# Mixture-of-experts weights: sixteen neighbouring rows of the gate and up matrices to a partition, in one 32 KB run

## What is computed

```
xn2 = rms_norm(x) * g_ffn
group  = argmax(softmax(xn2 @ w_router_group + b))            # 1 of 4 groups
e1, e2 = top2(softmax(xn2 @ w_router_expert + b) in group)    # 2 of its 8 experts
for each expert e, its tokens xb:                             # 32 experts
    hdn = silu(xb @ w_gate[e]) * (xb @ w_up[e])               # [2048 x 512] each, 4 MB each
    y   = hdn @ w_down[e]                                     # [512 x 2048], 4 MB
x += weighted sum of each token's two expert rows
```

## Time and profile before

| | us |
|---|---|
| median of 3 runs | 3235.22 |
| lowest, highest | 3231.18, 3235.81 |
| span of the profiled execution | 3231.3 |
| busy in the span: TensorE / VectorE / ScalarE | 2907.9 / 585.5 / 345.4 |

### The profile page before, as it was taken

How to read it: one execution, slowest core, us unless ns; L and a number is a source line. 1 busy time by engine, 2 the same in 40 slices (tenths; PEclk the granted TensorE clock), 3 DMA queues, 4 the chain that set the end, 5 groups by cost and what they waited for, 6 DMA issues and landing times.

```text
span 3231.3 us, 34069 instructions
## 1 busy us (share of the span) xinstructions
PE 2907.9 (90%) x14086; PEld 1892.7 (59%) x14086; DVE 585.5 (18%) x1118; ACT 345.4 (11%) x573; POOL 51.0 (2%) x76
## 2 busy tenths in 40 slices
PE   3989899999999999999999968888888888887697
PEld 2556565555555555555558865555545554554586
DVE  3243424224433000000000030000000000010311
ACT  2121121212222000000000010000000000000101
POOL 1000000000000000000000000000000000000000
PEclk8999999999999999999999969999999999999799
DMA  6252443322323333333333249999999999998422
GB/s 140 84 163 70 144 133 107 114 91 84 110 84 104 104 104 100 96 95 98 103 131 119 69 153 391 401 392 399 400 399 400 397 397 398 402 397 311 149 78 91
DMA packets 359592, 646.61 MB, mean 200 GB/s; under 512 B 7789, under 2 KB 196709, under 8 KB 340261
## 3 DMA queue, kind: packets, MB, share of 16 engines
q1 hardware_dynamic: 340944, 600.06, 52.0%
q0 software_dynamic: 6528, 27.54, 3.1%
q10 hardware_dynamic: 12090, 18.62, 1.6%
HBM read 616.16 MB, written 30.04 MB: 200 GB/s over the span
## 4 chain that ended last, share of the span: by engine, by line
PE 79%; DMA 14%; DVE 4%; issue 1%; ACT 1%; ACTq 0%; DVEq 0%; POOL 0%; POOLq 0%; SPq 0%
PE bank L1236 20%; PE bank L1135 13%; DMA arena<-in_w_exp_up_dram 12%; PE bank L1314 11%; PE bank L1206 8%; PE bank L1298 6%; PE bank L1348 5%; PE bank L1259 5%; PE bank L1332 4%; PE bank L1100 1%; DVE arena L886 1%; PE bank L1190 1%; DMA arena<-in_conv_r_w_dram 1%; PE bank L1350 1%; DMA arena<-in_state_ssm_dram 1%
## 5 line engine op out<-in xcount | busy, mean ns | idle before, releaser
L1236 PE MATMUL bank<-arena 128*128 128x384 f32 x2048 | 660.6, 486 | 0.0
L1314 PE MATMUL bank<-arena 128*64 128x256 f32 x4096 | 489.8, 402 | 109.6 <-DMA arena<-in_w_exp_up_dram 67.5
L1236 PEld LDWEIGHTS bank<-arena 128*128 128x128 f32 x2048 | 389.1, 190 | 271.4
L1314 PEld LDWEIGHTS bank<-arena 128*64 128x64 f32 x4096 | 313.2, 145 | 296.3 <-DMA arena<-in_w_exp_up_dram 74.7
L1135 PE MATMUL bank<-arena 128*128 128x384 f32 x1280 | 416.3, 488 | 0.0
L1135 PEld LDWEIGHTS bank<-arena 128*128 128x128 f32 x1280 | 243.9, 191 | 170.0 <-issue 3.3
L1206 PE MATMUL bank<-arena 128*128 128x384 f32 x1024 | 331.7, 486 | 3.0 <-ACT arena L570 3.0
L1206 PEld LDWEIGHTS bank<-arena 128*128 128x128 f32 x1024 | 194.3, 190 | 140.0 <-ACT arena L570 4.9
L1332 PE MATMUL bank<-arena 128*64 128x512 f32 x1024 | 230.1, 602 | 28.7 <-DVE arena L1046 25.1
L1298 PE MATMUL bank<-arena 128*128 128x128 f32 x1632 | 189.2, 278 | 9.2 <-DVE arena L1020 9.2
L1298 PEld LDWEIGHTS bank<-arena 128*128 128x128 f32 x1632 | 186.0, 194 | 15.5 <-issue 15.5
(11 more groups left out here) (287 smaller groups left out, 1350.5 us busy)
## 6 DMA issues: line engine op xcount, KB each, us to landing
arena<-in_w_exp_gate_dram SPq DMA_DIRECT2D x32, 4096.0 KB, 20.1
arena<-in_w_exp_up_dram SPq DMA_DIRECT2D x32, 4096.0 KB, 23.3
arena<-in_w_exp_down_dram SPq DMA_DIRECT2D x32, 4096.0 KB, 22.8
arena<-in_w_in_dram SPq DMA_DIRECT2D x48, 2048.0 KB, 8.3
arena<-in_w_out_m_dram SPq DMA_DIRECT2D x8, 2048.0 KB, 8.1
arena<-in_w_out_r_dram SPq DMA_DIRECT2D x8, 2048.0 KB, 8.1
arena<-in_w_o_dram SPq DMA_DIRECT2D x8, 2048.0 KB, 8.2
expert_rows<-arena ACTq DMA_DIRECT2D x64, 256.0 KB, 6.9
```

The lines of the kernel that those rows point to most:

```text
L1236: last = mm(banks[2 * s + cc][:, 0:T], slab[s % 2][:, k, cc * 128:(cc + 1) * 128], rhs[:, k, :], start=(k == 0), stop=(k == KC - 1))
L1314: last = mm(banks[2 * x + i][h * SLOTS:(h + 1) * SLOTS, 0:FF // 2], xe[:, k, x * SLOTS:(x + 1) * SLOTS], w[:, k, h * (FF // 2):(h + 1) * ( ...
```

## The change

Partition p now takes rows 16p to 16p+15 of the gate and up matrices, which lie next to each other in HBM: one run of 32 KB instead of 16 runs of 2 KB. The down matrix is loaded as before. Block k of the contraction then holds channels k, 16+k, 32+k and so on, so the tokens' channels must be permuted to match: the scaling of the three tiles of the second norm reads its source with a step of 16 elements (64 bytes) and writes in order; the gain g_ffn is loaded once more in the new order, by an eighth setup transfer, into `gffn_p`; the router's weights are loaded in the new order as well. The first and third norm are as before. The order of the waits and of the issues in `load_expert` is the same.

```diff
+        gffn_p = keep.take(KC)
...
             def load_expert(e, n):
 
-                for i, (dst, name) in enumerate(((w_gate, "w_exp_gate"), (w_up, "w_exp_up"), (w_down, "w_exp_down"))):
-                    sp.wait_ge(e_step, n * 4 + (1, 2, 4)[i])
-                    sp.dma_start(dst, a[name][0, ds(e, 1), :, :].rearrange("o (k p) c -> p (o k) c", p=128)).then_inc(ew_loaded[i], 16)
+                for i, (dst, name) in enumerate(((w_gate, "w_exp_gate"), (w_up, "w_exp_up"))):
+                    sp.wait_ge(e_step, n * 4 + (1, 2)[i])
+                    sp.dma_start(dst, a[name][0, ds(e, 1), :, :].rearrange("o (p k) c -> p (o k c)", p=128)).then_inc(ew_loaded[i], 16)
+                sp.wait_ge(e_step, n * 4 + 4)
+                sp.dma_start(w_down, a["w_exp_down"][0, ds(e, 1), :, :].rearrange("o (k p) c -> p (o k) c", p=128)).then_inc(ew_loaded[2], 16)
...
+            pool.dma_start(gffn_p, a["g_ffn"][0].rearrange("(p j) -> p j", j=KC)).then_inc(setup_in, 16)
...
-            pool.dma_start(w_r[:, :, EG:36], a["w_router_expert"][0].rearrange("(k p) c -> p k c", p=128)).then_inc(router_in, 16)
+            pool.dma_start(w_r[:, :, EG:36], a["w_router_expert"][0].rearrange("(p k) c -> p k c", p=128)).then_inc(router_in, 16)
...
-                TS(staging(n), src, rstd, None, ALU.mult).then_inc(n_scaled, 1)
+                if NT <= n < 2 * NT:
+
+                    TS(v3(staging(n), KC), src.rearrange("p (q j) -> p j q", j=KC), rstd, None, ALU.mult).then_inc(n_scaled, 1)
+                else:
+                    TS(staging(n), src, rstd, None, ALU.mult).then_inc(n_scaled, 1)
...
-            dve.wait_ge(setup_in, 16 * 7)
+            dve.wait_ge(setup_in, 16 * 8)
...
-                           spread(pcol[:, P_GFFN + 4 * b:P_GFFN + 4 * b + 4], 128), ALU.mult).then_inc(xe_evac, 1)
+                           spread(gffn_p[:, 4 * b:4 * b + 4], 128), ALU.mult).then_inc(xe_evac, 1)
```

More of the change, by code:

```diff
@@ L356, in _ @@
                 load_slab(1, a["w_o"], i * 512 + SLAB, wo_mm, 6 * i + 3)
-            w_gate, w_up, w_down = (v3(arena[:, 2 * i * SLABF:2 * (i + 1) * SLABF], n) for i, n in ((0, KC), (1, KC), (2, FC)))
+            w_gate, w_up = (arena[:, 2 * i * SLABF:2 * (i + 1) * SLABF] for i in range(2))
+            w_down = v3(arena[:, 4 * SLABF:6 * SLABF], FC)
             def load_expert(e, n):
-                for i, (dst, name) in enumerate(((w_gate, "w_exp_gate"), (w_up, "w_exp_up"), (w_down, "w_exp_down"))):
-                    sp.wait_ge(e_step, n * 4 + (1, 2, 4)[i])
-                    sp.dma_start(dst, a[name][0, ds(e, 1), :, :].rearrange("o (k p) c -> p (o k) c", p=128)).then_inc(ew_loaded[i], 16)
+                for i, (dst, name) in enumerate(((w_gate, "w_exp_gate"), (w_up, "w_exp_up"))):
[3 more added lines that the diff above has]
+                sp.dma_start(w_down, a["w_exp_down"][0, ds(e, 1), :, :].rearrange("o (k p) c -> p (o k) c", p=128)).then_inc(ew_loaded[2], 16)
             sp.wait_ge(wo_mm, 27)
@@ L472, in _ @@
                 pool.dma_start(p_in[:, t, :], src).then_inc(p_loaded, 16)
-            pool.dma_start(w_r[:, :, 0:EG], a["w_router_group"][0].rearrange("(k p) c -> p k c", p=128)).then_inc(router_in, 16)
-            pool.dma_start(w_r[:, :, EG:36], a["w_router_expert"][0].rearrange("(k p) c -> p k c", p=128)).then_inc(router_in, 16)
+            pool.dma_start(w_r[:, :, 0:EG], a["w_router_group"][0].rearrange("(p k) c -> p k c", p=128)).then_inc(router_in, 16)
+            pool.dma_start(w_r[:, :, EG:36], a["w_router_expert"][0].rearrange("(p k) c -> p k c", p=128)).then_inc(router_in, 16)
             pool.dma_start(rbias[:, 0:EG], a["b_router_group"][0].partition_broadcast(128)).then_inc(router_in, 16)
@@ L541, in _ @@
             act.wait_ge(consts_ready, CONSTS)
-            act.wait_ge(setup_in, 16 * 7)
+            act.wait_ge(setup_in, 16 * 8)
             act.wait_ge(dt_step, 1)
@@ L745, in norm_tile @@
                     TT(dst[:, 4 * b:4 * b + 4, t * 128:(t + 1) * 128], v3(banks[b][:, :], 4),
-                       spread(pcol[:, gain + 4 * b:gain + 4 * b + 4], 128), ALU.mult).then_inc(n_evac, 1)
+                       spread(gain[:, 4 * b:4 * b + 4], 128), ALU.mult).then_inc(n_evac, 1)
             dve.wait_ge(ptr_done, 1)
@@ L750, in _ @@
             for t in range(NT):
-                norm_tile(t, x_in[:, t, :], P_GMIX, xnT, t)
+                norm_tile(t, x_in[:, t, :], pcol[:, P_GMIX:P_GMIX + KC], xnT, t)
             dve.wait_ge(dt_done, 1)
-            dve.wait_ge(setup_in, 16 * 7)
+            dve.wait_ge(setup_in, 16 * 8)
             dve.wait_ge(consts_ready, CONSTS)
@@ L933, in _ @@
             for t in range(NT):
-                norm_tile(NT + t, x_res[:, t, :], P_GFFN, xn2T, t)
+                norm_tile(NT + t, x_res[:, t, :], gffn_p, xn2T, t)
             dve.wait_ge(router_in, 64)
@@ L1058, in _ @@
             for t in range(NT):
-                norm_tile(2 * NT + t, x_res[:, t, :], P_GPLE, xn2T, t)
+                norm_tile(2 * NT + t, x_res[:, t, :], pcol[:, P_GPLE:P_GPLE + KC], xn2T, t)
             with dve.Fori(0, 4) as i:
@@ L1110, in _ @@
             last.then_inc(dt_done, 1)
-            pe.wait_ge(setup_in, 16 * 7)
+            pe.wait_ge(setup_in, 16 * 8)
             for b in range(2):
```

## The result

The changed kernel takes 3179.19 us (median of 4 runs, 3173.25 to 3183.31) against 3233.2 for the kernel before on the same chip: ratio 0.9832, 95% interval 0.9818 to 0.9845. That is 54 us or 1.7% faster. The forecast was 3183, 52 us less.

The account below looks back on a forecast made before the run. The prediction took the experts' stage to be bound by DMA transfers, 65.8 us a pair. Longer runs save 59.5 us, less 4.5 for two limits meeting and 3.2 for scaling: 52 less, 3183 us, range 3164 to 3217.

Parts of the forecast that it names:

- The stage is bound by transfers: Experts' part: weight transfers and stores fill each pair's 65.8 us, 43.4 us of it depending on run length.
- The rate: Gate and up transfers: 32 KB runs save 0.96 us a matrix (0.85 to 1.06), 59.5 us over 62 transfers.
- rival D: Gate and up transfers: only part of 387 against 420 GB/s comes from run length; 26 us saved, 3212; chance 0.08.
- What the dry queue takes back: Single-buffered down issue: loop through TensorE (61.9 us) meets the DMA sum (62.0), costing 0.3 us a pair, 4.5 in all.
- The sum: Whole kernel: 59.5 - 4.5 - 3.2 = 52 us less, giving 3183 us.
- TensorE's slower stretch: Up matmuls after a wait, 8.81 instead of 7.1 us: this can vanish; up to 5 us at the low end.
- The scaling: Second norm on VectorE: reading in steps of 16 elements costs 1.06 us more each, 3.2 in all (0 to 8.3).
- Nothing on the path: Eighth setup transfer, router's weights, `gffn_p` and stores cost nothing; stores land in about 22 us instead of 6.9, hidden.
- A: Gate and up transfers: 32 KB runs read worse, at 360 GB/s 53 us slower, 3289 or more; chance 0.11.
- B: Gate and up transfers: runs cut again or limit elsewhere, rate stays 387 GB/s, 3238, no change; chance 0.06.
- C: Experts' loop: TensorE's side decides, 63.1 us a pair, gain 2.7 a pair and 42 in all, 3196; chance 0.20.

## Why the prediction was right, step by step

- **The stage is bound by transfers, and 43.4 us of a pair hang on the length of the runs.** Shown: with less of TensorE's work the kernel before gains 0.2 us a pair, and cutting the changed kernel's runs to 2 KB at the same addresses takes the period back to 65.6.
- **The rate.** I took 0.96 us a matrix, between 0.85 (nothing gained above 8 KB) and 1.06 (the straight line). At 432 GB/s a matrix takes 9.71 us, 1.13 saved: the line was right out to 32 KB (1.22 us for a packet, measured 1.21), and 62 transfers are worth 70 us, not 59.5. This term was too small by about 10. The page "DMA: Bandwidth & Descriptors" of the Trainium skill (Why small descriptors are slow) gives, as an estimate, 4.5% for 2 KB. Measured it is 387 against 432, 10%, so the packet costs about twice what the page gives, and rival D falls.
- **What the dry queue takes back.** I had seen that both limits meet at 62 us and took 0.3 a pair. The transfers saved 4 x 1.13 = 4.52 a pair and the period fell by 3.23, so 1.3 was lost, 19 us over 15 pairs instead of 4.5. The mechanism was right and its size wrong, by about 15. The experiments agree with the size: early issue of half of the down matrix gives 1.10 us a pair, and less work on TensorE 1.2 to 1.5. What I had not seen is that the queue also comes back slowly. From 2.5 to 6.5 us behind the late down issue the engines are busy again (share 0.98, mean of 14 pairs) but move 377 GB/s; in the kernel before they move 412 there, at 1.02. Why isn't shown.
- **The sum.** The two errors, 10 and 15 us, have opposite signs. That 3183 lies within 4 us of the measured time is luck to that extent; the mechanism isn't.
- **TensorE's slower stretch.** I had left up to 5 us for it at the low end of the range. The up matmuls of the second expert take 7.13 us where the granted clock is 1.00 (2024.05 to 2031.18) and 8.81 where it is 0.81 on average (2211.88 to 2220.69), that is, partly at the lower of its two levels. On the chain 6 of 16 such groups take 7.13 in the changed kernel and 2 of 16 before; all 16 together take 131.5 us instead of 141.8. They lie in the loop that decides after the change, so some of these 10 us are in the gain; no run isolates how much.
- **The scaling.** 1.96 us instead of 1.29, 0.67 more in each of three tiles, 2.0 instead of 3.2. From the first of these scalings to the first gate matmul the path grew by 0.8 only (70.1 to 70.9 us). The rule of the page "SBUF — State Buffer" of the Trainium skill (Door 1) on 16-byte lines speaks of a penalty here; on VectorE it is small (the step is no slower than L1053, 2.35 us for the same size, in order), on TensorE's weight loads it is large (194 to 311 ns).
- **Nothing on the path.** The setup transfer shows nowhere: the first instruction behind it still waits 10.6 us for the dt matmuls, as in the earlier trace rows. The stores take longer to land, 11.6 us (median) instead of 6.9; I had 22 as the most. No wait of ScalarE for them appears.
- **Rivals.** A (long runs read worse) and B (cut again) fell with the first window at 428 GB/s in packets of 32 KB. C was in part true: the period of 62.59 lies between my 62.3 and C's 63.1, and after the change TensorE's side of the loop costs 1.2 to 1.5 us a pair, but the total, 54 us faster, lies with the forecast and not with C's 39.

What stays open: of the 5 us between the changed kernel and the one with halves issued late, how much is due to the 16 KB runs of down and how much to the order of TensorE's work wasn't separated.

## What to carry to other kernels

Where a stage is bound by transfers, compare the rate in windows with short and with long runs; two rates give a fixed cost for each packet, and here it could be extrapolated by a factor of four. When transfers get faster and a buffer has no second copy, look at once for the issue that now comes too late: giving back half of the buffer earlier brought another 17 to 18 us here, and 22 with the longer runs of down and the other order. And if a permutation has to be paid, pay it where the data passes once (three scalings on VectorE, 2 us) and not in an operand that is loaded again and again (weights of TensorE, 160 us).

## What the runs showed of the hardware

- Touching pieces in an access pattern are merged when the program is built, and one packet then carries 32 KB.
- On the sync engine's queue the rate from HBM into 128 partitions is 387 GB/s with runs of 2 KB, 420 with 8 KB and 432 with 32 KB (428 in a window of 16 us); the stage's mean is 399, 412, 417 and 419 with 2, 8, 16 and 32 KB for gate and up.
- A weight load of TensorE (128x128, fp32) takes 311 ns with a step of 64 bytes between elements and 194 in order; VectorE's scaling of 128x2048 takes 1.96 us instead of 1.29.
- When a down matrix is issued only as the queue runs dry, the 6 us around the issue have 303 GB/s (mean of 14 pairs), against 412 with half of it issued earlier.
- Stores that share the DMA engines with packets of 32 KB land in 11.6 us instead of 6.9, and nothing waited for them here.
